# Small statistics moved from VectorE to ScalarE, key products laid among the key pairs, and an earlier last transpose of the time mix

## What is computed

```python
def _rwkv7_step(S, inp):
    r, w, k, v, a, b = inp
    sa = jnp.einsum('bhvk,bhk->bhv', S, a)
    S = S * w[:, :, None, :] + sa[..., None] * b[:, :, None, :] + v[..., None] * k[:, :, None, :]
    y = jnp.einsum('bhvk,bhk->bhv', S, r)
    return S, y
...
    mean = jnp.mean(y, axis=-1, keepdims=True)
    var = jnp.mean(jnp.square(y - mean), axis=-1, keepdims=True)
    yn = ((y - mean) * lax.rsqrt(var + LNX_EPS)).reshape(B, T, D) * lnx_w + lnx_b
    bonus = (jnp.sum(rh * kh * r_k, axis=-1, keepdims=True) * vh).reshape(B, T, D)
    out = ((yn + bonus) * g).astype(x.dtype)
    return out @ w_o
```

## Time and profile before

| what | value |
|---|---|
| time, median of 3 runs | 1098.86 us (1093.63 to 1102.5) |
| time of the profiled execution | 1091.18 us |
| its span from first to last instruction | 1089.3 us |
| mean granted TensorE clock | 0.997 of full |
| PE busy | 1062.2 us, 98% of the span |
| DVE, ACT, POOL busy | 798.9, 604.0, 219.3 us |

### The profile page before, as it was taken

How to read it: one execution, slowest core, us unless ns; L and a number is a source line. 1 busy time by engine, 2 the same in 40 slices (tenths; PEclk the granted TensorE clock), 3 DMA queues, 4 the chain that set the end, 5 groups by cost and what they waited for, 6 DMA issues and landing times.

```text
span 1089.3 us, 18693 instructions
## 1 busy us (share of the span) xinstructions
PE 1062.2 (98%) x7143; PEld 917.0 (84%) x7143; DVE 798.9 (73%) x1103; ACT 604.0 (55%) x928; POOL 219.3 (20%) x234
## 2 busy tenths in 40 slices
PE   7999998999999999999999999999999999999997
PEld 6997797888888888789888888998777789888886
DVE  7997878778886658777788756688867776666643
ACT  6766363555564566856666554635665446555532
POOL 0125493121221011002222200571100001122200
PEclk9999999999999999999999999999999999999999
DMA  8553172646666466345667575556452555766552
GB/s 249 172 172 117 39 244 69 175 135 181 187 192 253 167 151 162 121 131 150 187 189 192 194 271 158 159 191 215 154 136 84 194 162 131 193 191 193 193 193 78
DMA packets 219747, 183.11 MB, mean 168 GB/s; under 512 B 43265, under 2 KB 197614, under 8 KB 219678
## 3 DMA queue, kind: packets, MB, share of 16 engines
q1 hardware_dynamic: 215710, 171.43, 52.4%
q0 software_dynamic: 3392, 8.66, 2.5%
q10 hardware_dynamic: 576, 2.07, 0.5%
HBM read 179.44 MB, written 2.69 MB: 167 GB/s over the span
## 4 chain that ended last, share of the span: by engine, by line
PE 80%; DVE 13%; issue 2%; DMA 2%; ACT 1%; POOL 1%; SPq 1%; DVEq 0%; POOLq 0%; ACTq 0%
PE bank L288 20%; PE bank L282 13%; PE bank L284 13%; PE bank L283 13%; PE bank L289 10%; DVE ring L417 3%; PE bank L295 2%; PE bank L1250 2%; DVE arena L1687 1%; DVE arena L1782 1%; DVE stat L1780 1%; PE bank L375 1%; PE bank L2167 1%; DMA arena<-in_kv_w_up 1%; PE bank L1365 1%
## 5 line engine op out<-in xcount | busy, mean ns | idle before, releaser
L417 DVE TENSOR_TENSOR ring<-ring,arena 128x2048 fp32r<-128x2048 f32 (+1 forms) x138 | 312.9, 2271 | 112.4 <-ACT arena L411 110.8
L282 PE MATMUL bank<-arena 128*128 128x512 f32 (+3 forms) x980 | 343.6, 351 | 3.7 <-DVE ring L417 3.0
L288 PE MATMUL bank<-arena 128*128 128x512 f32 x960 | 335.7, 396 | 0.0
L411 ACT ACTIVATE arena<-ring 128x2048 fp32r<-128x2048 f32 (+1 forms) x145 | 272.1, 1879 | 98.0 <-DMA ring<-in_ffn_w_out 42.9
L289 PE MATMUL bank<-arena,ring 128*128 128x256 f32 x960 | 267.2, 278 | 0.0
L284 PE MATMUL bank<-arena 128*128 128x512 f32 (+3 forms) x720 | 264.7, 368 | 0.0
L283 PE MATMUL bank<-ring,arena 128*128 128x512 f32 (+2 forms) x560 | 216.1, 386 | 0.0
L288 PEld LDWEIGHTS bank<-arena 128*128 128x128 f32 x960 | 180.1, 188 | 42.6
L282 PEld LDWEIGHTS bank<-arena 128*128 128x128 f32 x980 | 185.4, 189 | 29.2 <-issue 5.4
L289 PEld LDWEIGHTS bank<-arena,ring 128*128 128x128 f32 x960 | 180.6, 188 | 0.0
L284 PEld LDWEIGHTS bank<-arena 128*128 128x128 f32 x720 | 135.6, 188 | 22.2
(11 more groups left out here) (338 smaller groups left out, 1274.9 us busy)
## 6 DMA issues: line engine op xcount, KB each, us to landing
ring<-in_ffn_w_in SPq DMA_DIRECT2D x80, 512.0 KB, 5.1
ring<-in_ffn_w_out SPq DMA_DIRECT2D x44, 512.0 KB, 4.4
ring<-in_w_gate_up SPq DMA_DIRECT2D x40, 512.0 KB, 5.1
ring<-in_w_in SPq DMA_DIRECT2D x18, 1024.0 KB, 5.1
ring<-in_a_w_rkv SPq DMA_DIRECT2D x12, 1024.0 KB, 5.4
ring<-in_w_down SPq DMA_DIRECT2D x22, 512.0 KB, 3.7
ring<-in_a_w_o SPq DMA_DIRECT2D x4, 1024.0 KB, 6.8
arena<-in_ffn_w_in SPq DMA_DIRECT2D x8, 512.0 KB, 4.7
```

The source lines that it names most:

```text
L282: nc.tensor.matmul(dst, stationary[0], moving[0], start=start, stop=False)
L288: nc.tensor.matmul(dst[:, :], stationary[0], both_parts, start=start, stop=False)
L411: nc.scalar.activation(buf(hi_of(n), 0, w, arena12), ring[:, r, 0:w], ACT.Copy).then_inc(hi_ready, 1)
L417: on.tensor_tensor(ring12[:, r, 0:w], ring[:, r, 0:w], buf(hi_of(n), 0, w, arena12).bitcast(F32), ALU.subtract).then_inc(split_ready, 1)
```

## The change

It has six edits; only the last reaches beyond the time mix:

1. `key_values(0)` and `key_values(1)` no longer follow the sixteen key pairs; they stand behind pair 9 and pair 12.
2. The two halves of `value_means` become one reduction over both chunks on DVE and one scaling of 32 columns on ACT, behind the copy that turns the inverses around.
3. `variance` is split: DVE keeps the reductions (`squares_summed`), ACT makes the multiply and add. DVE does the first reduction ahead of the `state_added` sums, and both `gated_out(0, q)` behind the last sum of the sweep.
4. POOL starts `values_centred(1)` only when DVE has split the first `w_o` slot (`split_ready`), and thus also what follows on POOL.
5. PE makes both second inverses before `o_turn(0, 0)`, and `o_turn(1, 1)` before tile (1, 0) of `w_o` and not before (1, 1). DVE splits the last `w_o` slot before `gated_out(1, 0)`.
6. `early_lo(dve, 0, 0)` leaves its place between the last two `o_lo` for the place of `early_lo(dve, 0, 1)`, which moves behind `turn_dve` of chunk 0.

`gated_out` itself, where the root is multiplied in, is the same in both kernels.

```diff
@@ ffn_front_dve
             if f != 1:
+                early_lo(dve, f, 0 if f == 0 else 1)
+            turn_dve(dve, turn, 0, 4, hi, lo)
+            if f == 0:
                 early_lo(dve, f, 1)
-            turn_dve(dve, turn, 0, 4, hi, lo)
             post_scale(dve, i, 1)
@@ rwkv_pe
-            pe.wait_ge(v_evac, 4)
-            key_values(0)
-            key_values(1)
+            for l in range(PAIR_BANKS):
+                if l >= 4:
+                    pe.wait_ge(prod_evac, PAIR_BANKS + l - 3)
+                pairs(l, key, l // 8).then_inc(prod_mm, 1)
+                if l == 9:
+                    pe.wait_ge(v_evac, 4)
+                    key_values(0)
+                elif l == 12:
+                    key_values(1)
...
             block_inverses(1, 0)
+            block_inverses(1, 1)
             o_turn(0, 0)
-            block_inverses(1, 1)
...
                 elif (a, s) == (1, 0):
+                    o_turn(1, 1)
                     pe.wait_ge(o_split, 3)
-                elif (a, s) == (1, 1):
-                    o_turn(1, 1)
@@ rwkv_act
             def squares(a, q):
                 act.wait_ge(ymm, 2 * a + q + 1)
-                if a == 1:
-                    act.wait_ge(var_ready, 2 + q + 1)
                 nc.scalar.activation(y_squared[q], bank[Y_BANK[a][q]][:, :], ACT.Square).then_inc(squared, 1)
+
+            def variance(a, q):
+                stat = slice(a * H + 8 * q, a * H + 8 * (q + 1))
+                act.wait_ge(stats_ready, 2 + 2 * a + q + 1)
+                nc.scalar.activation(y_var[:, stat], y_sq[:, stat], ACT.Copy, bias=LNX_EPS, scale=1.0 / N).then_inc(var_ready, 1)
...
+            act.wait_ge(stats_ready, 1)
+            nc.scalar.activation(v_mean, v_sum, ACT.Copy, scale=-1.0 / N).then_inc(stats_ready, 1)
...
             squares(0, 0)
+            act.wait_ge(state_mm, 1)
+            ahead(act, FIRST["w_o"] + 1, split_act)
+            variance(0, 0)
             squares(0, 1)
+            variance(0, 1)
...
             squares(1, 0)
+            squares(1, 1)
             o_evac(0, 1)
-            squares(1, 1)
+            variance(1, 0)
+            variance(1, 1)
@@ rwkv_dve
-                link(dve, nc.vector.tensor_reduce(y_sq[:, stat], by_head(y_squared[q]), AX, ALU.add))
-                nc.vector.tensor_scalar(y_var[:, stat], y_sq[:, stat], 1.0 / N, LNX_EPS, ALU.mult, ALU.add).then_inc(var_ready, 1)
+                nc.vector.tensor_reduce(y_sq[:, stat], by_head(y_squared[q]), AX, ALU.add).then_inc(stats_ready, 1)
...
-            for a in range(NT):
-                value_means(a)
+            nc.vector.tensor_reduce(v_sum, by_head(buf(W_V)), AX, ALU.add).then_inc(stats_ready, 1)
...
+            squares_summed(0, 0)
             state_added(0)
             state_added(1)
-            variance(0, 0)
+            squares_summed(0, 1)
             block_added(1, 0, 1)
-            variance(0, 1)
             block_added(1, 0, 2)
             block_added(1, 1, 1)
-            gated_out(0, 0)
             block_added(1, 0, 3)
             block_added(1, 1, 2)
             block_added(1, 1, 3)
+            gated_out(0, 0)
             gated_out(0, 1)
...
+            ahead(dve, LAST["w_o"], split_dve)
             gated_out(1, 0)
-            ahead(dve, LAST["w_o"], split_dve)
             gated_out(1, 1)
             o_lo(1, 0)
-            early_lo(dve, 0, 0)
             o_lo(1, 1)
@@ rwkv_pool
             rest_gated(0)
+            pool.wait_ge(split_ready, SPLIT_NO[FIRST["w_o"]] + 1)
             values_centred(1)
```

30 lines of the change are left out of this document (11 added, 19 removed).

## The result

The changed kernel takes 1091.67 us in the median of 20 runs (1087.74 to 1096.19), the kernel before, on the same chip, 1099.91 us in the median of 20 (1093.63 to 1103.65). The ratio is 0.993, with a 95% interval of 0.9915 to 0.9945: faster by 0.7%, or 8 us, where 1099.5 was forecast with a lower end of 1093. The profiled execution of the changed kernel took 1092.61 us, 0.9 from its median. Laid side by side, the two profiles show a loss of 1.4 us, not a gain of 8.

What follows compares the result with a forecast made beforehand. PE, busy 98% of the span, was taken as the bound, with about 5.5 us of waits in reach. Shifts carried along PE and DVE ended at +0.65 us, added to the 1098.86 median: 1099.5 us, range 1093 to 1104.

Steps and rivals of the forecast that it cites:

- the base of the sum: Whole kernel: local +0.65 us added to the profiled 1091.18, then carried to the median of runs shown, 1098.86, giving 1099.5 us.
- chunk 1 of x: End of the mix: chunk 1 of x reaches the waiting PE 0.65 us later, after the moved early splits.
- nothing there gives time back, so this stays to the end: FFN 0: PE is busy 179.89 of 180.00 us, so the +0.65 us lasts to the end.
- `steps`: Behind the key pairs: start moves to 137.4, +1.0 us, as the last pair's mask and copy now stand last.
- second inverses: PE's `block_inverses`: late blocks pass through DRAM later and come last, at 151.3, +1.9 us; bounds +1.0 and +2.1.
- `o_turn(1, 0)`: Among the `w_o` tiles: PE must wait for DVE's `gated_out(1, 0)` until 188.0, where it stood at 185.75 before.
- `o_turn(1, 1)`: End of the mix: follows tile (0, 3) at 191.35 instead of 192.70, -1.35 us for all that hangs on it.
- L518: DVE's chain at the mix's end: -1.35 plus the second early split's 2.28 us makes it +0.93 us.
- the 11.0 us allowed for DVE: DVE's splits, reductions, `o_lo` and `gated_out(1, 0)`, from 177.0 to 188.0, ahead of `o_turn(1, 0)`.
- the one expensive row on the path: Statistics: L1805, a DVE multiply and add of 8 columns at 161.20, takes 2.36 us beside POOL's L1944.
- rival b: After PE's new waits ahead of `steps` and the inverses, a second half-clock stretch loses 1.2 us: 1100.8 us; chance 0.10.
- the lowest, 1098.0: Rival: the front costs nothing, as hidden waits take the products and late blocks land in time; about -0.9 us; chance 0.22.

Runs made afterwards that it cites:

- the wait's one number: Kernel before with one number changed: POOL's centring waits for both value means, not the first; 1092.82 us, ratio 0.9952.
- the loads on SP: Kernel before with the two broadcast loads of the gains issued by SP instead of POOL; 1091.97 us, ratio 0.994.
- the end order: Kernel before with only the order at the end of the mix changed (edits 5 and 6); 1097.09 us, ratio 0.996.
- the first profile of before: The unchanged kernel before, in the profiled execution the prediction started from; 1091.18 us.
- the second profile of before: The unchanged kernel before, run and profiled again; 1100.87 us over 10 runs, profiled execution 1101.8 us.
- 20 trials of the sequence: Small kernel, not the real one, repeating POOL's and DVE's sequence at the value means; these trials have two load issues ahead of the product; kernel time 647.92 us.
- the small kernel: Not the real kernel: POOL issues one or two loads, then two products and a clearing, while DVE's scaling comes later from trial to trial; 640.93 us.

## Why the prediction was wrong

**The step that failed** is the base of the sum: "the sum is 1091.18 + 0.65 = 1091.8 us against the profiled execution; that one lies 7.7 us below the median of the runs shown, so the forecast in their terms is 1098.86 + 0.65". The 7.7 us were carried over as a constant. They were for the most part a wait that the profiled execution happened not to have, and that the change removes. An execution 7.7 us below the median shown, and 2.5 below the lowest of the three runs, should have been a question: what does an ordinary execution have that this one lacks? The trace gave a hint: L1841 had lasted 0.17 and 1.18 us for the same 16 columns, and the prediction priced only the 2.36 us of L1805 and the 3.53 of L417 as meetings with POOL. L1841 was not in its list of terms.

The sum in that execution's own terms, 1091.8, is within 0.2 us of the changed kernel's median, and that is luck. The profile of after reached chunk 1 of x 0.24 us early, not 0.65 late, and what followed moved it by -2.1, +2.5 and +1.3. The step "nothing there gives time back, so this stays to the end" was too strong as well: at 353.7 a wait took back a lead of 2.5 us.

**What ordinary executions have**, shown in the kernel: a scaling shut out for 7.19 us, a wait of PE of 5.7, the clock at half for 6.8 us from within that wait. Three different edits take it away and recover nearly the same, as differences of medians against the runs of before on the same chip: the wait's one number (6.5 us), the scaling on ACT (5.7), and the loads on SP (7.2). By their ratios they are 5.3, 4.5 and 6.6, each known to about 2.7 either way, so the three can't be told apart. Together with the end order, the one number gives the whole of the change's gain.

**How the change does it**: edit 2 leaves no small operation on DVE there, and POOL waits for ACT's scaling between its issues and its product, 1.57 us in the profile of after. Either alone would do: the run with edit 2 alone has no such wait, and the run with edit 2 undone has both scalings on DVE and keeps a wait of 0.46. "Small operations off VectorE" names the edit, and the cause is a meeting that depends on when the engines arrive.

**The local steps**, as shifts against the first profile of before, were mostly right:

| step | predicted | measured |
|---|---|---|
| `steps` | 137.4 (+1.0) | 138.49 (+2.0) |
| second inverses | 151.3 (+1.9) | 151.42 (+2.0) |
| state products | +1.25 | +1.29 |
| first sum of the sweep | 163.6 (0.0) | 163.60 |
| last sweep | -0.3 | -0.3 |
| first tile of `w_o` | 177.3 (+0.75) | 177.33 |
| `o_turn(1, 0)` | 188.0 | 187.41 |
| `o_turn(1, 1)` | 191.35 (-1.35) | 190.66 (-2.0) |
| L518 | +0.93 | +0.14 |
| chunk 1 of x | +0.65 | -0.24 (L537, 206.56 to 206.32) |

`steps` was under-sized: the last pairs end at 137.5, not 136.5, and the step that moving the products in "leaves the end of all of it at 136.5" was wrong. The clock is not the cause, as it was low from 128.0 to 131.4 in both profiles. At the full level the twelve pair records behind a key product take 1.92 us up to the next product (132.47 to 134.39), where twelve of an unbroken run take 1.6, as in the second profile of before (48 up to the products at 133.30):

```profile
126.92 6.44 PE L1250 MATMUL bank<-arena 64*128 64x256 f32 x48 [1.94 <-ACT arena L1620]
```

Why the broken run is slower stays open. The second row of the table is right for another reason than the one given: PE has no wait ahead of the second inverses at 151.42, and the 2.0 us are those of `steps`. The late blocks, taken as last, were there: SP, which waits for the first chunk's before it issues the second's, issued those at 151.01. The last four are forecast 0.6 to 0.9 us too late: the 11.0 us allowed for DVE from 177.0 on took 10.6 from 176.83, to the start of `o_turn(1, 0)` at 187.41, and L518 waited for nothing behind the second split.

**The statistics** (edits 3 and 4), taken in the prediction for the one expensive row on the path, show no gain: 1092.57 (ratio 0.9918) with edit 3's small operations back on DVE, and the one number with the end order reaches the changed kernel's time without edits 3 and 4. Edit 4 and DVE's new order were not undone by themselves.

**Edits 5 and 6** were mis-sized in ordinary executions, where about 0.8 us was expected of them alone. They bring 4.0 us by the medians (1101.09 to 1097.09) and 4.4 by the ratio. On top of the one number it is 3.2 by the medians (6.5 to 9.7) and 1.6 by the ratios (0.9952 to 0.9937), in the changed kernel 2.9 by the ratios; the intervals hold all of these, so the size is open between 1.6 and 4.4. The waits for x explain 1.1 to 2.0 of it: the 2.0 ahead of chunk 0's transposes goes, and 0.9 ahead of chunk 1's comes in (none in the profile with edits 5 and 6 alone). Another part is the fall of the clock for 3.4 us behind that wait of 2.0, which the prediction had only as a harm that the change might bring (rival b). It costs 1.2 us by the prediction's own price from the earlier trace rows, and past it the shift of the second profile of before goes from 6.1 to 7.6. The first profile had the same wait and no fall behind it.

**Of the rivals** none was right, as all of them were reckoned from the same base; the lowest, 1098.0, lay above every run of the changed kernel. The sentence that a time below 1090 "would mean that something outside 124 to 214 moved" had the wrong place: the effect lay inside, in executions that had not been looked at.

**The Trainium skill** (SBUF — State Buffer, "Who interferes with whom") has the lock held for one whole instruction by whoever starts first. The runs agree where no issue stands ahead (1.50 to 1.91 us beside a product of 1.9), and go beyond it: behind an issue without a pause, the scaling stays out over three of POOL's instructions, until the last of them ends.

## What to carry to other kernels

Before a sum is made, ask whether the profiled execution is an ordinary one: where its time is outside the runs, profile again and compare operation by operation, since a gap of some microseconds may be a single wait. Look for a small VectorE operation that lasts as long as a GpSimd one beside it, and for a load issued by GpSimd directly ahead of GpSimd work; a wait between the two, or another queue for the load, ended it here. When such a meeting decides the time, a small shift of arrivals can be worth most of an edit (here a wait of 0.37 us was worth 6.5), so undo the edit's parts one at a time before the gain is ascribed.

## What the runs showed of the hardware

- A GpSimd load issue followed without a pause by products and a clearing keeps a 16-column VectorE scaling out until the last of them ends: 7.2 us in the kernel and 6.9 to 7.2 in 20 trials of the sequence. A pause of 0.03 us instead of 0.02 between them ends it, and the scaling goes from 6.96 to 1.54. Still open: in the first profile of before the scaling begun 0.77 us into the product lasted 1.18 us with the same issues just ahead; in the small kernel the same distance gave 6.51.
- Even without an issue, a clearing directly behind a product prolongs the lock-out (4.48 us for 3.60 + 0.95, and 4.18 for a scaling begun 1.2 us into a product of 4.5), while between two products the small operation gets in. An operation with two operands in SBUF waits for the product alone (3.59).
- FFN loops run at two paces in different executions of the same code, PE busy throughout: between 231 and 338 us the matmuls of the changed kernel's first profile drew ahead of those of before from 0.6 to 2.5 us, and those of its second profile not at all; in the second profile of before they fell behind from 8.5 to 10.6 between 902 and 1028. What sets the pace stays open.
- The clock's falls for 3.4 or 6.8 us came in or behind PE's waits of 1.8 to 2.0 and of 5.7 us, but not with all: two profiles (edit 1 undone, and the one number changed) had waits of 1.8 to 2.0 and no fall before the program's last 6 us, and the wait of 2.2 at 353.7 in the profile of after was followed by none.
